# Chunked delta-rule scan on Trainium2: four 64x64 quarters of TensorE in turn, inverse blocks read two steps ahead, and work moved between three queues

## The reference

```
# S_t = S_{t-1} diag(w_t) + (S_{t-1} a_t) b_t^T + v_t k_t^T ;  y_t = S_t r_t
def step(S, inp):
    r_t, w_t, k_t, v_t, a_t, b_t = inp
    sa = einsum('bhij,bhj->bhi', S, a_t)
    S = S * w_t[:, :, None, :] + sa[..., :, None] * b_t[..., None, :] \
        + v_t[..., :, None] * k_t[..., None, :]
    return S, einsum('bhij,bhj->bhi', S, r_t)
wkv = scan(forward) + scan(reverse)
```

## Time and profile before

| | |
|---|---|
| median of 3 runs | 2507.27 us (2507.16 to 2508.43) |
| the profiled execution's own time | 2509.72 us |
| its span, first to last instruction | 2508.0 us |
| TensorE busy over the span | 2328.4 us, 93% |
| VectorE, ScalarE, GpSimd busy | 73%, 48%, 28% |
| mean granted TensorE clock | 0.971 of full speed |

### The profile page before, as it was taken

The page is one execution under the profiler, slowest core; times in us unless marked ns, Lnnn a source line. Parts: engine busy times, 40 slices in busy tenths (PEclk is TensorE's granted clock), DMA queues, the critical chain, the costliest instruction groups (busy, mean ns, idle before and its releaser), DMA issues. The chain is left out here.

```text
span 2508.0 us, 50080 instructions
## 1 busy us (share of the span) xinstructions
PE 2328.4 (93%) x19504; PEld 2035.2 (81%) x19504; DVE 1827.3 (73%) x2480; ACT 1208.3 (48%) x1748; POOL 709.5 (28%) x715
## 2 busy tenths in 40 slices
PE   6899999999996999996989896699999999999997
PEld 4788888888876898986767674699999999999996
DVE  5547888988865676675767677677777777777777
ACT  6355454445522334432335332566565666666656
POOL 2234242433412444454453534011011111101111
PEclk9999999999997999998999998799999999999998
DMA  4335253442537766763647352777777777777777
GB/s 151 85 96 162 86 161 116 137 149 87 172 114 226 210 188 188 192 173 79 234 128 258 111 202 101 301 246 256 264 256 245 237 258 255 251 251 260 264 256 245
DMA packets 294772, 479.74 MB, mean 191 GB/s; under 512 B 142224, under 2 KB 209952, under 8 KB 266832
## 3 DMA queue, kind: packets, MB, share of 16 engines
q1 hardware_dynamic: 275552, 412.52, 50.1%
q0 software_dynamic: 7760, 27.08, 4.8%
q10 hardware_dynamic: 11296, 37.82, 4.6%
HBM read 363.51 MB, written 110.69 MB: 189 GB/s over the span
## 5 line engine op out<-in xcount | busy, mean ns | idle before, releaser
L2751 PE MATMUL bank<-e_xt,e_w_high 128*128 128x384 f32 x1792 | 524.7, 357 | 3.7 <-DVE e_xt L2919 2.1
L2906 DVE TENSOR_TENSOR e_w_low<-e_w,e_w_high 128x2048 fp32r<-128x2048 f32 x192 | 436.2, 2284 | 69.2 <-ACT e_w_high L2807 69.2
L2752 PE MATMUL bank<-e_xt,e_w_low 128*128 128x192 f32 x1792 | 449.1, 251 | 0.0
L2807 ACT ACTIVATE e_w_high<-e_w 128x2048 fp32r<-128x2048 f32 x192 | 366.4, 1908 | 107.8 <-PE bank L2773 79.2
L2752 PEld LDWEIGHTS bank<-e_xt,e_w_low 128*128 128x128 f32 x1792 | 342.2, 191 | 0.6
L2751 PEld LDWEIGHTS bank<-e_xt,e_w_high 128*128 128x128 f32 x1792 | 338.1, 189 | 5.5 <-issue 2.5
L462 PE MATMUL bank<-h_high,w_high 128*128 128x512 f32 x864 | 258.0, 407 | 1.5 <-DVE work L872 1.5
L855 DVE SCALAR_TENSOR_TENSOR work<-work,vec 128x1551 f32<-128x1551 f32 x116 | 243.8, 2102 | 2.4
L465 PE MATMUL bank<-h_low,w_high 128*128 128x512 f32 x864 | 244.8, 391 | 0.0
L468 PE MATMUL bank<-h_high,w_low 128*128 128x512 f32 x864 | 243.7, 390 | 0.0
L2685 POOL DMA_INDIRECT xacc_dram<-e_y,e_put x30 | 47.3, 1576 | 651.9 <-DVE e_y L2941 647.3
(11 more groups left out here) (356 smaller groups left out, 5168.7 us busy)
## 6 DMA issues: line engine op xcount, KB each, us to landing
e_w<-in_ew SPq DMA_DIRECT2D x192, 1024.0 KB, 5.9
features_dram<-work SPq DMA_DIRECT2D x48, 512.0 KB, 3.3
fe<-features_dram SPq DMA_DIRECT2D x24, 1024.0 KB, 8.1
x_w<-in_w_mix SPq DMA_DIRECT2D x48, 512.0 KB, 5.1
w<-in_w_in ACTq DMA_DIRECT2D x35, 512.0 KB, 3.6
ba_tok_dram<-work SPq DMA_DIRECT2D x96, 128.0 KB, 2.2
gates_dram<-work ACTq DMA_DIRECT2D x16, 768.0 KB, 4.5
all<-ba_tok_dram SPq DMA_DIRECT2D x96, 128.0 KB, 3.4
```

Source lines behind the costliest of these rows:

```text
L2751: nc.tensor.matmul(*wide, start=(k == 0), stop=False)
L2752: nc.tensor.matmul(*narrow, start=False, stop=False)
L2807: nc.scalar.activation(w_high[n % RING][:], w[n % RING][:], ACT.Copy).then_inc(w_high_done, 1)
L2906: tt(w_low[n % RING][:], w[n % RING][:], w_high[n % RING][:].bitcast(F32), ALU.subtract)\
```

## The change

In short:

- **Quarters.** Every 64x64 product is written so that the directions alternate inside the loop over head pairs, and direction 1 sends rows 0 to 63 to output partitions 64 to 127 and the reverse. Four matmuls in a row are then in four different quarters. `products` becomes `products_wide` (64x128, five steps ahead, `FIRST`) and `products_narrow` (64x64). `solve`, `level_n` and `level_x` take both directions in one call. `full` and `state` keep their shapes.
- To bring the swapped halves back, ScalarE copies some results of direction 1 as two half copies (`swapped`).
- **TensorE's order** is state of chunk i - 2 (both), level_n 0, solve, level_x 0, narrow, full(0), wide, level_n 1, full(1), products_c, level_x 1.
- **GpSimd** takes `levels` over from VectorE, as two operations of 128x128 a direction, ahead of each `expand`, and the additions and multiplications of `conv`; the pair (i + 3, i + 4) is inverted after the expands of an odd i, and the last pair is no longer inverted by halves.
- **Queues.** ScalarE's queue issues direction 1's G stores and diagonal loads, in the middle of its copies; `compact` is issued two steps ahead, and is three transfers instead of one for direction 1.
- The ring of `ALL` has 6 buffers instead of 5. The order of b and a in direction 1's tokens is reversed in DRAM (the line in `project`).

The diff, cut to its core:

```diff
-                            out = g.ba_tok[d, tok(b), r, hp, 1 - j, :]
+                            out = g.ba_tok[d, tok(b), r, hp, j if d else 1 - j, :]
...
-    LEVELS, AHEAD, RING = 2, 4, 5
+    LEVELS, AHEAD, FIRST, RING, RING_ALL, PARTS = 2, 4, 5, 5, 6, 3
...
+        HALF = [ROWS, ROWS[::-1]]
...
+        def lower(eng, d, i):
+            eng.wait_ge(v_g[d], i + 1)
+            out = g.g_dram[d, i, :].rearrange("(h r e) -> h r e", h=HP, r=2)[:, :, 0:HD * CH]
+            for r in range(2):
+                eng.dma_start(out[:, r, :].rearrange("h (t c) -> t h c", c=CH), ALL[d][i % RING_ALL][ROWS[r], :, G_[d], :])\
+                   .then_inc(g_out[d][i % 2], 16)
+        def diagonal(eng, d, i):
+            m = i // 2
+            if m >= 2:
+                inverted(eng, m - 2)
+            eng.wait_ge(g_out[d][i % 2], 32 * (i // 2 + 1))
...
+        def compact(eng, d, i):
...
+            if d == 0:
+                eng.dma_start(XC[d][i % 2][:].rearrange("p h x c -> p h (x c)"), src).then_inc(l_x[d][i % 2], 16)
+            else:
+                eng.dma_start(XC[d][i % 2][:, :, 0, :], src[:, :, 0:BASE]).then_inc(l_x[d][i % 2], 16)
+                for out, r in zip(ROWS, HALF[d]):
+                    eng.dma_start(XC[d][i % 2][out, :, 1, :], src[r, :, BASE:2 * BASE]).then_inc(l_x[d][i % 2], 16)
...
                 for i in range(NCH):                          # SyncE
                     if i == 0:
+                        lower(sp, 0, FIRST - 1)
+                    if i + FIRST - 1 < NCH:
+                        diagonal(sp, 0, i + FIRST - 1)
+                    if i % 2 == 0 and 2 <= i < NCH - AHEAD - 2:
+                        features((i + AHEAD + 2) // 2)
+                    if i % 2 == 0 and i < NCH - 2:
+                        inverses((i + 2) // 2)
                     if 1 <= i < NCH - 1:
                         tokens(i + 1)
+                    if i + 2 < NCH:
+                        for d in DIRS:
+                            compact(sp, d, i + 2)
                     if 1 <= i < NCH - 1:
                         keys(i + 1)
+                    if i + FIRST < NCH:
+                        lower(sp, 0, i + FIRST)
                     if 1 <= i < NCH - 1:
                         values(i + 1)
...
                 def body(i):                                  # TensorE
                     post, pre = i >= 1, i + AHEAD < NCH
+                    if i >= 2:
+                        for d in DIRS:
+                            state(d, i - 2)
+                    level_n(i, 0)
                     if post:
+                        solve(i - 1)
+                    level_x(i, 0)
+                    if pre:
+                        products_narrow(i + AHEAD)
                     if post:
                         full(0, i - 1)
+                    if i + FIRST < NCH:
+                        products_wide(i + FIRST)
+                    level_n(i, 1)
                     if post:
                         full(1, i - 1)
                     if pre:
+                        products_c(i + AHEAD)
+                    level_x(i, 1)
...
                 for i in range(NCH):                          # ScalarE
+                    if i >= 2:
+                        for d in DIRS:
+                            out(d, i - 2)
                     if i >= 1:
                         for d in DIRS:
                             solved(d, i - 1)
+                    for side in range(2):
                         for d in DIRS:
+                            level_x(d, i, 0, side)
+                    if i >= 2:
+                        for d in DIRS:
+                            store(d, i - 2)
+                    if i + FIRST - 1 < NCH:
+                        lower(act, 1, i + FIRST - 1)
+                    if i + AHEAD < NCH:
+                        for d in DIRS:
+                            receptance(d, i + AHEAD)
+                    if i + FIRST - 1 < NCH:
+                        diagonal(act, 1, i + FIRST - 1)
                     for d in DIRS:
+                        level_x(d, i, 1, d)
...
+                def levels(d, i):                             # GpSimd
+                    if i >= 2:
+                        pool.wait_ge(m_n[d], (i - 1) * LEVELS)
+                    pool.wait_ge(v_g[d], i + 1)
+                    for n, blocks in enumerate((slice(1, None, 2), slice(2, None))):
+                        part = lambda v: v.rearrange("p h (b c) -> p h b c", c=BASE)[:, :, blocks, :]
...
                 for i in range(1, NCH - 1):
                     for d in DIRS:
+                        levels(d, i + 1)
+                    for d in DIRS:
                         expand(d, i + 1)
-                    if i % 2 == 0 and i + 4 < NCH:
-                        invert((i + 2) // 2)
+                    if i % 2 == 1 and i + 3 < NCH:
+                        invert((i + 3) // 2)
+                    conv(i)
...
                 for i in range(NCH):                          # VectorE
                     post, pre = i >= 1, i + AHEAD < NCH
-                    level_n(0, i, 0)
+                    level_n(i, 0)
...
+                    if i >= 2:
+                        for d in DIRS:
+                            carried(d, i - 2)
+                    if pre:
+                        for d in DIRS:
+                            masked_narrow(d, i + AHEAD)
                     aside(i)
                     if post:
                         summed(0, i - 1)
+                    level_n(i, 1)
                     if post:
                         summed(1, i - 1)
                     if pre:
                         for d in DIRS:
                             masked_c(d, i + AHEAD)
+                    if i + FIRST < NCH:
+                        for d in DIRS:
+                            masked_wide(d, i + FIRST)
```

More of the change, by code:

```diff
@@ L1167, in _ @@
                 tokens(0)
+                lower(sp, 0, 2)
                 inverses(0)
+                for i in range(2):
+                    compact(sp, 0, i)
+                lower(sp, 0, 3)
+                for i in (2, 3):
+                    diagonal(sp, 0, i)
                 keys(0)
                 values(0)
-                compact(0)
-                compact(1)
-                for d in DIRS:
-                    lower(d, 3)
-                diagonal(2)
-                diagonal(3)
@@ L1485, in _ @@
                         receptance(d, j)
+                    if j % 2 == 1:
+                        for i in (j - 1, j):
+                            lower(act, 1, i)
+                        for i in (j - 1, j):
+                            diagonal(act, 1, i)
+                for i in range(2):
+                    compact(act, 1, i)
                 for i in range(NCH):
+                    if i >= 2:
+                        for d in DIRS:
+                            out(d, i - 2)
                     if i >= 1:
@@ L1508, in _ @@
                         root()
+                for d in DIRS:
+                    out(d, NCH - 2)
+                    store(d, NCH - 2)
                 for d in DIRS:
@@ L1776, in _ @@
                         summed(0, i - 1)
-                    if pre:
-                        masked(0, i + AHEAD)
-                    for d in DIRS:
-                        level_n(d, i, 1)
-                    if i + 1 < NCH:
-                        levels(1, i + 1)
+                    level_n(i, 1)
                     if post:
@@ L1797, in _ @@
                     carried(d, NCH - 1)
-                for q in range(QT):
-                    joined(q)
 def mixing(nc, a, g):
```

589 lines of the change are left out of this document (276 added, 313 removed).

## The result

The changed kernel takes 2526.6 us (median of 4 runs, 2524.8 to 2527.0) against 2507.2 for the kernel before: a ratio of 1.0075, with an interval from 1.0057 to 1.0092. It is 19 us slower, where 14 us faster was predicted. The profiled execution after has a span of 2523.0 us against 2508.0.

The account below looks back on a forecast made before the run. TensorE's work and the diagonal blocks' way bound a step almost equally; afterwards the inversion's chain. 801.7 + 306 + 3.8 put step 21 at 1111.5, 13 us earlier; with 1 us of tail, 2507.3 becomes 2493, range 2455 to 2517.

Parts of the forecast that it names:

- Quarters: TensorE's 64x64 products: four at once instead of two halve 10.6 us a step to 5.3, 9.7 with full and state.
- The chain: From an odd step's level_n through summed, receptance, diagonal load, inversion, levels and expands: 30.6 us a pair; chance 0.52.
- The clock: TensorE at half clock for about 5 us after each idle, in twelve or so patches of 3 to 5 us.
- TensorE's own way through both is about 24.5 us: TensorE's work through a pair of scan steps, taken as shorter than the 30.6 us the pair was to last.
- the sum: Start 801.7, ten pairs 306 and centring 3.8 put step 21 at 1111.5; with the tail, 14 us saved in all.
- the 6 us that it was to idle for GpSimd: TensorE's wait before each odd step's level_n, for GpSimd's expand, about 6 us a pair.
- The estimate of 12 to 13 us a step: Step length left by VectorE's and ScalarE's orders if the inversion is not in the way.
- the 2437 rival: Inversion not in the way: 12 to 13 us a step, 70 us saved over twenty steps, 2437; chance 0.08.
- about the same: SyncE's load: it loses two G stores and a load and gains two of compact, so no change was expected.
- 3.8 us for the centring: VectorE's six centre operations ahead of summed(0) in step 19 were to add 3.8 us to that pair.
- The slower rival: Diagonal blocks' way longer through levels, load landing and inversion: 33.6 us a pair, 2523; chance 0.18.
- the tail: VectorE's variance, extra and normalise in steps 21 and 22, 15.5 us each as before; 1 us was to be saved.

Follow-up runs that it names:

- e15: e7 with the steady loop's feature loads cut to 64 columns of one head pair (values left out): 2481.9 us, ratio 0.9905.
- e7: The changed kernel with GpSimd's levels and expands of two steps ahead of the inversion and a new order on SyncE: 2508.8 us, ratio 1.0017.
- e18: The changed kernel with e7's order on SyncE alone, GpSimd's order kept: 2510.4 us, ratio 1.0021.
- e13: e7 with the 128-column products of solve and wide each split into two of 64 columns: 2544.6 us, ratio 1.0164.
- e10: e7 with each head's two products in state merged into one with 128x128 weights: 2537.2 us, ratio 1.0129.

## Why the prediction was wrong

- **Quarters: right.** 32 records of 64 columns take 0.69 us with the last one's end, the first of the next group starts 0.52 after the first, and the busy time fell by 73 us. The size was too hopeful: the work was put at 9.7 us a step, and TensorE is busy for 12.0 in after and for 11.3 in e15, where the clock is nearly full. The Trainium skill, "TensorE: Matmul & The Clock Gate", part 3, The mechanism, says that a weight load overlaps running matmuls only where the row group differs. The trace does not bear it out here: with two of four products in each row group the pace of 32 records is 0.52 us, against 1.08 before.
- **The chain: right in its order and almost in size.** GpSimd waits 82.2 us in 10 turns for gb, ScalarE's receptance for fu. The second half of the pair measured 15.9 (15.8). The first half measured 16.4, not 14.8: ScalarE's blocks landed in 3.6 us instead of 2.6 over the scan, and unnamed waits lengthened the step's first half. Clock patches are there (0.57 from 1069 to 1077).
- **The clock: there, but no run takes it apart from the waits.** About twelve patches at half clock were foreseen, and twelve lie between steps 1 and 21, though of 3.4 to 13.7 us, 68 us together (a granted clock of 0.90). The same TensorE instructions are busy for 193.0 us in e7 at 0.91 and for 180.1 in e15 at 0.98. The unnamed waits are idle time like any other, so they may cost more than their own length; that was not tested.
- **The step that failed: "TensorE's own way through both is about 24.5 us".** That counted columns and took the supply of instructions as free. In after a pair has 23.9 us of busy TensorE and 5.7 us of unnamed waits, which the sum put at nothing, and the 6 us that it was to idle for GpSimd are 1.5. With the queues out of the way (e7) a pair takes 31.8 us: 24.1 busy, 6.4 in unnamed waits, 1.1 in named ones; without the feature loads (e15) it takes 28.2. Against the 32.1 of before, nearly nothing was left to win, whatever the chain did. The estimate of 12 to 13 us a step, and with it the 2437 rival, was out of reach: 50 rounds in 16 steps are 3.1 a step, and at e15's 4.5 us each they are 14.1 us.
- **SyncE's queue: "about the same" was wrong.** I counted its issues and not its order. Features ahead of the inverse store made the store's landing 7.6 us instead of 2.6, compact held the queue for 33.7 us, and what stood behind came late, among it the second direction's y for step 19. With e18's order step 21 begins 13 us earlier: 1.2 by step 1, 3.3 between steps 1 and 3, 6.5 between steps 19 and 21, and only 2.0 in the sixteen steps between. The order costs at both ends and hardly in the middle. The sum had 3.8 us for the centring; steps 19 to 21 took 40.5 where 34.4 were foreseen.
- **The slower rival** put the pair at 33.6 us and gave 2523, near what was measured, but that is luck: it put the loss into the blocks' way. There a levels operation took 0.46 us and not 0.73, and the inversion 11.1 and not 12.8. The pair measured 32.2, and e18 shows that the blocks' way can be shortened without a gain in the steps.
- **The sum.** Step 21 was foreseen at 1111.5 and came at 1137.9. The 26.4 us are: 3.1 by step 1, 4.2 in the first pair, 13.0 in the eight that follow, 6.1 in the last. Behind it the tail grew by 1.6 where it was to lose 1, and the profiled execution lies 1.8 below its median and not 2.4 above, which makes up the 33 us between 2493 and 2526.6. (Two slips in the working change nothing: the diagonal load's line adds up to 14.7 and not 14.8, and the chances to 0.20 for the same and 0.16 for slower.)

Shown are SyncE's order (e18 alone gives 13.5 us back) and that TensorE stops at every 256 instructions or a multiple, with rounds of mostly 4.2 to 4.9 us (e15's rows and counts, e13's waits). That a fetch is what these rounds wait for rests on the packets' places, on e13, whose waits grew with the instructions, and on e10, whose waits fell with them; no run could change the fetches alone.

## What to carry to other kernels

Before counting on small products side by side, divide the number of TensorE's instructions by 256 and multiply by the usual round seen in a trace (4.4 us here, with single ones down to 3.5): a step that is to fall below that needs fewer instructions first, and products of 64 columns on half an array already stand close to it. When a queue is rearranged, follow what lands behind what: a large load put just ahead of a small store that others wait for costs at each wait that follows in the same queue. And when one chain explains the time, look for the second limit before sizing the gain; here the chain was to give 30.6 us a pair, and TensorE with its stops takes 28 to 32 without it.

## What the runs showed of the hardware that was not expected

- TensorE stops in the middle of a group at every 256 instructions or a multiple, for up to 4.3 us in after, when these took less than about 4.4 us; each stop ends 1.2 to 1.6 us after a 16 KB packet of the instruction queue. In 800 to 1125 us that is 53.5 us after, 7.4 before, 0.7 in the kernel before without feature loads.
- A round with 2 MB of loads in flight took 7.61 us instead of 4.19. Its packet began 5.3 us into the round and not 1.6, and took no longer (0.9 us).
- A product with 128x128 weights costs nearly twice what its two halves of 128x64 cost: in state 79.0/573 = 0.138 us a record (e10), against 2 x 43.3/1152 = 0.075 us (e7).
- The same TensorE instructions took 193.0 us of busy time at a granted clock of 0.91 (e7) and 180.1 at 0.98 (e15).
